# A two-layer mixer and mixture-of-experts trunk: smaller last block, both gates in the rows, twelve converted experts, and plain gathers at the second layer's start

## The reference

```python
def reference(x, ...):                      # x: (4, 4096, 1024) float32
    for l in range(DEPTH):                  # DEPTH = 2
        m = hybrid_mixer(x, ...)            # x @ w_in -> 2048 columns; four groups:
                                            #  gated 128-chunk mixing, 31-tap causal conv,
                                            #  trailing means of 2,4,8,16, 3-tap gated conv;
                                            #  RMS norm per group of 256, then @ w_o
        x = layer_norm(ALPHA * x + m, ln1_g[l], ln1_b[l])
        f = grouped_moe(x, router_w, router_b, exp_w_gate[l], exp_w_up[l], exp_w_down[l])
        x = layer_norm(ALPHA * x + f, ln2_g[l], ln2_b[l])
    return x

def grouped_moe(...):
    # 16 experts in 4 groups; the best group by the sum of its two best scores,
    # the top 2 experts in it, gates = softmax of their two logits
    for e in range(16):
        h = silu(xt @ w_gate[e]) * (xt @ w_up[e])      # 1024 -> 512
        y = y + dense_gates[:, e:e+1] * (h @ w_down[e])  # 512 -> 1024
```

## Time and profile before

| | |
|---|---|
| median of 3 runs | 2028.21 us (2025.96 to 2029.23) |
| profiled execution, time | 2037.57 us |
| its slowest core (core 2), span | 2036.5 us |
| the other cores' spans | 2007.5 to 2031.0 us |
| mean granted TensorE clock | 0.81 to 0.82 of full speed |
| busy share of the span | PE 62%, VectorE 51%, ScalarE 31%, GpSimd 24% |
| DMA moved | 334.99 MB, mean 164 GB/s |

### The profile page before, as it was taken

The page is one execution under the profiler, slowest core; times in us unless marked ns, Lnnn a source line. Parts: engine busy times, 40 slices in busy tenths (PEclk is TensorE's granted clock), DMA queues, the critical chain, the costliest instruction groups (busy, mean ns, idle before and its releaser), DMA issues.

```text
span 2036.5 us, 23801 instructions; the slowest of 8 cores (2007.5 to 2036.5 us)
## 1 busy us (share of the span) xinstructions
PE 1260.2 (62%) x7040; PEld 640.8 (31%) x7040; DVE 1041.5 (51%) x2328; ACT 637.1 (31%) x1109; POOL 496.1 (24%) x361
## 2 busy tenths in 40 slices
PE   0577868586429698685254687767535967878200
PEld 0433333232215454342121233333223534544000
DVE  1357486757733232232279658675761322323597
ACT  0344544435202222120254254443421211211122
POOL 4011315041340000001845112303031000000597
PEclk9897879798659899897567798978766989989655
DMA  9947667759848999997965878974124999997663
GB/s 199 260 137 99 99 94 125 104 89 180 160 123 208 260 224 249 246 236 222 206 134 64 112 93 115 125 89 90 63 84 144 236 244 230 247 256 168 225 210 131
DMA packets 78766, 334.99 MB, mean 164 GB/s; under 512 B 10776, under 2 KB 22688, under 8 KB 62880
## 3 DMA queue, kind: packets, MB, share of 16 engines
q0 software_dynamic: 26384, 166.16, 50.1%
q1 hardware_dynamic: 52240, 167.14, 25.3%
HBM read 362.71 MB, written 147.19 MB: 250 GB/s over the span
## 4 chain that ended last, share of the span: by engine, by line
PE 38%; DMA 17%; DVE 16%; issue 15%; ACT 8%; POOL 3%; DVEq 0%; SPq 0%; ACTq 0%; another core or an unknown queue 0%; POOLq 0%
PE pb L596 36%; DMA yg<-s_scr 6%; DMA s_wbuf<-ew 3%; DMA s_xy<-xg 3%; DMA s_xtok<-x 2%; ACT s_scr L605 2%; PE pT L1287 1%; ACT s_xy L641 1%; DVE s_sm L624 1%; ACT L605 1%; ACT s_xtok L605 1%; DVE s_scr L609 1%; DVE s_sm L675 1%; DVE s_scr L616 1%; DVE s_xtok L609 1%
## 5 line engine op out<-in xcount | busy, mean ns | idle before, releaser
L596 PE MATMUL pb<-s_xy,s_wbuf 128*128 128x352 bf16 (+2 forms) x2992 | 657.4, 349 | 145.2 <-ACT s_scr L605 34.5
L596 PEld LDWEIGHTS pb<-s_xy,s_wbuf 128*128 128x128 bf16 x2992 | 288.6, 104 | 396.3 <-issue 237.0
L596 PE MATMUL pb<-s_wbuf,s_scrb 128*128 128x512 bf16 (+1 forms) x768 | 232.1, 399 | 51.6 <-DMA s_wbuf<-ew 28.4
L616 DVE TENSOR_SCALAR s_scr<-pb,s_gsl 128x512 f32<-128x512 f32 (+1 forms) x192 | 135.6, 745 | 234.8 <-PE pb L596 167.6
L596 PE MATMUL pb<-s_wbuf,s_xy 128*128 128x512 bf16 x792 | 239.2, 412 | 8.9 <-DVE s_xtok L624 2.2
L609 POOL TENSOR_TENSOR s_xtok<-s_xtok,s_lnp 128x1024 f32<-128x1024 f32 x76 | 183.8, 2422 | 199.8 <-ACT s_xtok L605 153.4
L609 DVE TENSOR_TENSOR s_scrb<-s_scr,pb 128x352 bf16<-128x352 f32 x128 | 64.6, 519 | 229.9 <-PE pb L596 218.8
L406 POOL DMA_DIRECT2D s_wbuf<-exp_w x42 | 22.4, 532 | 645.8 <-PE pb L596 577.8
L641 ACT COPY s_xy<-pT 128x1024 bf16<-128x1024 bf16 (+1 forms) x96 | 90.3, 940 | 283.4 <-PE pT L1287 253.2
L1287 PE MATMUL pT<-s_identb,s_xy 128*128 128x128 bf16 (+1 forms) x768 | 121.9, 226 | 89.0 <-DMA s_xy<-xg 53.2
L709 PE MATMUL pT<-s_identb,s_scr 128*128 128x128 bf16 x336 | 55.0, 273 | 182.2 <-ACT s_scr L605 70.5
(11 more groups left out here) (119 smaller groups left out, 1619.2 us busy)
## 6 DMA issues: line engine op xcount, KB each, us to landing
ew<-exp_w POOLq DMA_DIRECT2D x36, 1536.0 KB, 17.8
s_wbuf<-ew SPq DMA_DIRECT2D x54, 1024.0 KB, 14.6
s_wbuf<-exp_w POOLq DMA_DIRECT2D x42, 1024.0 KB, 15.4
yg<-s_scr SPq DMA_DIRECT2D x64, 512.0 KB, 15.0
s_xy<-xg SPq DMA_DIRECT2D x32, 514.0 KB, 13.4
yg<-s_scr SPq DMA_DIRECT2D x32, 384.0 KB, 17.8
xg<-s_gov SPq DMA_DIRECT2D x2, 5808.0 KB, 31.4
s_xtok<-x SPq DMA_DIRECT2D x17, 512.0 KB, 10.6
```

What stands on the lines that cost most here:

```text
L596: em.op(PE, lambda e: e.matmul(out.ap, lhsT.ap, rhs.ap, start=start, stop=stop), w=[out], r=[lhsT, rhs])
L616: em.op(E, lambda e: e.tensor_scalar(out=out.ap, in0=a.ap, scalar1=a1, scalar2=None, op0=op0), w=[out], r=rr)
```

## The change

Four things are changed together.

1. The blocks become 384 (halo tile and two more), 512, 512, 512 and 256 tokens. In the second layer the first block is no longer cut down: its convolutions, pooling and projections run on all 384 columns, while `G_section`, `O0_section`, `A_section` and `R_section` take only its tiles 1 and 2 (`tiles_of`).
2. The rows of `xg` carry three float32 columns: the second gate, the difference of first and second gate, and the base slot of the first expert. They are written once per block, and all scatters of the block follow with no write between them. `x_turn` works out the gate of a slot by two VectorE operations (is the first expert this one? then add the difference) in place of one copy. Rows are loaded with 516 float32 words instead of 514.
3. `PRE` becomes every expert with e % 4 != 3: twelve instead of nine (5, 9 and 13 are new), in both layers. `NTOK` becomes 3, and a conversion counts 4 instead of 6 bytes an element in the scheduler's DMA model.
4. In the second layer, tiles 0 to 3 are gathered with eight plain gathers into four buffers in the `w_o` region of `wbuf` and added by `vt` (VectorE or GpSimd). The load of `w_o` (piece 4) moves behind them into the second layer's program; the pieces 0 to 3 stay at the end of the first.

```diff
-MBLOCKS = [(0, 128)] + [(128 + i * NB, NB) for i in range(TM // NB)]
+MBLOCKS = [(0, 384), (384, NB), (896, NB), (1408, NB), (1920, 256)]
-PRE = [e for e in range(NE) if e % 2 == 0 or e == 1]
+PRE = [e for e in range(NE) if e % 4 != 3]
-NTOK = 2
+NTOK = 3
...
-                       w=[ewD[l].rows(2 * e + h, 2 * e + h + 1), tok[k].rows(0, 1)], r=after, size=64 * 12288 * 6)
+                       w=[ewD[l].rows(2 * e + h, 2 * e + h + 1), tok[k].rows(0, 1)], r=after, size=64 * 12288 * 4)
...
+            def tiles_of(b):
+                t0, nb = MBLOCKS[b]
+                return list(range(1 if last and b == 0 else t0 // 128, (t0 + nb) // 128))
...
+                ts(DVE, gcol(0), c1(lb), -0.5, ALU.mult, 0.5, ALU.add)
+                cpy(DVE, gcol(1), c1(lb))
+                tt(DVE, v16(tmp), v16(eq1), e16(ebase()), ALU.mult)
+                rsum(la, tmp)
+                cpy(DVE, gcol(2), c1(la))
...
                 for k in range(2):
-                    xr, xf = xrow[b == nblk - 1], xrowf[b == nblk - 1]
-                    gcol = xf(0, nt * GW // 2).v(lambda ap: ap.rearrange("p (t c) -> p t c", t=nt)[:, :, D // 2:D // 2 + 1])
-                    gcol.box = xr[0](D, GW).box[:3] + (xr[nt - 1](D, GW).box[3],)
-                    cpy(DVE, gcol, ge.v(lambda ap: ap[:, k * nt:(k + 1) * nt].rearrange("p (t o) -> p t o", o=1)))
                     for t in range(nt):
...
             if l > 0:
+                stg = [View(wbuf, 16384 + k * 2 * D, F32, D) for k in range(4)]
+                for i in range(4):
+                    for k in range(2):
+                        c, g = k * NT + i, stg[(2 * i + k) % 4]
+                        gc = gai(2 * i + k, 2 * i + k + 1)
+                        em.gather(g().ap, ygD[l - 1].ap, gc.ap, "dg%d" % c, w=[g(), gtok.rows(i, i + 1)],
+                                  r=[ygD[l - 1].rows(0, NSLOT + 1), gc])
+                    for k in range(2):
+                        vt(xtile(i), stg[(2 * i + k) % 4](), xtile(i), ALU.add)
+                load_layer_weights(l, only=[4])
                 for (t0, nb) in MBLOCKS:
                     for k in range(2):
-                        for i in range(t0 // 128, (t0 + nb) // 128):
+                        for i in range(max(4, t0 // 128), (t0 + nb) // 128):
                             c_gather(k, i, ygD[l - 1])
...
-                gv = xgG[s](j * 514 + 512, j * 514 + 513)
-                cpy(DVE, gsl(s * CT + j, s * CT + j + 1, 0, nj), gv.v(lambda ap: ap[0:nj, :]))
+                gv = [xgG[s](j * 516 + 512 + q, j * 516 + 513 + q).v(lambda ap: ap[0:nj, :]) for q in range(3)]
+                gs_ = gsl(s * CT + j, s * CT + j + 1, 0, nj)
+                stt(DVE, gs_, gv[2], float(e * CAP), gv[1], ALU.is_equal, ALU.mult)
+                tt(DVE, gs_, gs_, gv[0], ALU.add)
...
-                load_layer_weights(l + 1)
+                load_layer_weights(l + 1, only=range(4))
```

More of the change, by code:

```diff
@@ L880, in build @@
             last = (l == n_layers - 1)
+            def tiles_of(b):
+                t0, nb = MBLOCKS[b]
+                return list(range(1 if last and b == 0 else t0 // 128, (t0 + nb) // 128))
             def G_section(b):
                 t0, nb = MBLOCKS[b]
[L883 to L884 removed]
+                tiles = tiles_of(b)
                 GS = 272
@@ L961, in CPS_section @@
                 t0, nb = MBLOCKS[b]
-                tiles = list(range(t0 // 128, (t0 + nb) // 128))
-                state_only = last and b == 0 and stop is None
                 accs = []
@@ L1225, in R_section @@
                     ts(DVE, flag(l, l + 1), m1.v(lambda ap: ap[:, 0:1]), float(CAP), ALU.is_gt)
-            skip0 = last and stop is None
             def C_section(b):
```

115 lines of the change are left out of this document (46 added, 69 removed).

## The result

The change makes the kernel slower. Its median is 2072.45 us (2066.89 to 2076.43, 4 runs) beside 2027.39 us for the kernel before (4 runs): a ratio of 1.022, 95% interval 1.0194 to 1.0245. The forecast was 1956 us, with a chance of 0.08 for slower. Some executions of a kernel run longer at a lower granted clock; medians and ratios here leave them out, which leaves e3 and e11 two runs and no interval, while the stage times of e5 come from such an execution, and the ratios of e13 to e16, which count one of the kernel before (2055.8 us), would be 0.003 higher without it. The slowest core is now core 5.

What follows compares the result with a forecast made beforehand. Expert stages were taken as near DMA and PE limits, mixers as bound by the PE, ACT and DVE chain. Terms -14 - 12 - 19 - 27 - 0 = -72 us, from 2028.2 to 1956 us; range 1920 to 2002.

Steps and rivals of the forecast that it cites:

- the price of the pace: Both mixers: cost of planning a conversion at 11.7 us; 5 us in the first mixer, hidden in the second.
- 200 us are free: hidden: Second mixer: DMA is busy 0.65 of 584 us, so six more conversions, 79 us per layer, cost nothing.
- the first rival: Conversions planned at 11.7 us but taking 13.2 block the POOL queue: 80 us in all, 2036 us, chance 0.08.
- The conversion's 13.2 us: DMA time of one conversion, worked out from the software queue's busy time with 12 us taken off for scatters.
- 430 to 450 us of work in 417: First mixer: conversions, scatters and loads exceed the time left, so 15 to 35 us spill into the first expert stage.
- Part 1 and 2, first mixer, -14 us: First mixer: blocks and gates save 23 us in the tail, less loading, router and conversion costs; bounds 0 and -30.
- Part 3, expert stages, -12 and -27 us: Expert stages: three more converted experts give -27 us each, less 15 us of spill in the first.
- Part 4 and the second mixer, -19 us: Second mixer: plain gathers and a fuller first block end the stage at 1526 against 1545; bounds +10 and -45.
- The first norm begins near 968: Start of the second layer: plain gathers and two adds let the first norm begin near 968 instead of 987.1.
- The second mixer gains nothing: Rival for the second mixer: DVE sets its pace, 1975 us in all, chance 0.15.
- The turnover of `wbuf`: Rival: it holds the expert stages, not DMA; -10 and 0 instead of -27 and -12, 1985 us, chance 0.17.
- the fourth rival: The expert stages come down to PE's floor: -40 in the second, -30 in the first, 1925 us, chance 0.15.

Runs made afterwards that it cites:

- e3: The changed kernel with a conversion counted as 6 bytes an element again, still twelve experts and three tokens: 2032.7 and 2034.2 us, no interval.
- e11: e5 with twelve converted experts in the second layer and nine in the first: 1966.5 and 1986.1 us, no interval.
- e5: e1 with the second layer's gathers put back to accumulating ones, so new blocks and gates only: 1978.5 us, ratio 0.975 to the kernel before.
- e13: The kernel before with only the planned cost of a conversion changed, 4 in place of 6: 2093.2 us, ratio 1.029.
- e16: e12 with the staged gathers as well, their adds and norms fixed on VectorE: 1951.6 us, ratio 0.960.
- e1: The changed kernel with part 3 undone (nine converted experts, two tokens, factor 6): 2016.5 us, ratio 0.989 to the kernel before.
- e4: The changed kernel with two tokens instead of three: 2091.3 us, ratio 1.024 to the kernel before.
- e8: The changed kernel with twelve tokens and twelve semaphores instead of three tokens: 2220.2 us, ratio 1.096 to the kernel before.
- e10: The kernel before with only the gates in the rows, on its old blocks and gathers: 1990.7 us, ratio 0.981.
- e9: The changed kernel with nine converted experts instead of twelve, keeping factor 4 and three tokens: 2086.7 us, ratio 1.030 to the kernel before.
- e12: e10 with twelve converted experts in the second layer only, factor 6 and two tokens: 1973.2 us, ratio 0.971 to the kernel before.
- e14: The changed kernel with a planned conversion cost of 5 in place of 4: 2003.0 us, ratio 0.985 to the kernel before.

## Why the prediction was wrong

By stage, the forecast was -14, -12, -19 and -27 us. The medians of the cores moved by +41, -45, +63 and -37. Both mixers went the other way, and the expert stages gained more than was forecast.

**The step that failed** is the price of the pace, which the sum put at 5 us for both mixers together. It stands in three places: "a price for the conversions on the POOL queue (part 3), 5 us" in the first mixer, "200 us are free: hidden" for the second, and the first rival, at 80 us in all and a chance of 0.08. The mechanism of that rival is what happened: POOL waits for conversions, and "the norm's multiplies, the adds and the scatters" stand behind. Measured, the two mixers lose 64 and 53 us to part 3 (after against e1), 117 in all; the planned cost alone, on the kernel before, costs 43 and 26 (e13). The rival's price was 1.5 us of lag for each of 52 conversions, and the trace shows 14.4 us for a planned 11.7: 2.7 us each, 140 us in all. That this is near 117 is not a confirmation of the sum, since POOL's waits were 369 us and only part of them reached the mixers. The two arguments against the rival fail. It names "three tokens instead of two": that does nothing (e4), and twelve are worse (e8). That "the real mixer gives more time than a plan without waits" was not enough: in e13 POOL waits 229 us. Free time of the DMA engines, counted over a stage, hides this: the second mixer's share was 0.65, and still only 0.73 in the changed kernel, where q0 is at 98% while conversions run.

**The conversion's 13.2 us** were worked out from a queue that was not full. In the full queue it is 14.2 us of DMA time and 14.4 from start to start with no scatter between, so the price itself was 1 us too low. By the Trainium skill (DMA: Bandwidth & Descriptors, Bandwidth) an estimate for its 4.7 MB is 13.2 us; the trace of the changed kernel is 8% above that. The sum that gave 430 to 450 us of work in 417 left out the 19 us of first expert pieces that it names: its terms give 450 to 470, and a spill of 32 to 52 us by its own numbers.

**Part 1 and 2, first mixer, -14 us.** Without part 3 it is -24 (e1), inside the bounds, but the sum was made of wrong terms. The gates were put at 11 us and give 21 (e10). The wider first and smaller last block were put at 8 net and give 2, which is nothing. The step looked at the tail alone and left out POOL's 7 us of wait for the same write in another block.

**Part 3, expert stages, -12 and -27 us.** The second's 27 is right in size: 29 against e9, 19 for e12 against e10. In the first the spill did not come with factor 4: the last conversion was issued at 557 us and the stage began only at 636, as the mixer had grown. The gain there was 24 against e9. With factor 6 the spill is real: e3's first expert stage is 391 us, 24 above the kernel before and 32 above e1. Some 7 us of the whole change's gain in this stage belong to part 4.

**Part 4 and the second mixer, -19 us.** The stage is 10 us longer without part 3 (e1). The earlier start of the gathers, put at 6.4 us, came true at 7 us. "The first norm begins near 968" was right in its start (18.7 us after the first gather in e1, for 25.7 before) and wrong in what follows: the norm's multiply was taken to be free to run, and stands on POOL behind the gathers. That tiles 0 to 3 come first was taken from the code; the planner mixes the order. The gates give 17 us there, where 3 were counted, since POOL's 18 us of waits in the middle blocks were left out; this hides how much the gathers cost.

**Beside the rivals.** "The second mixer gains nothing" holds for e1, and DVE's pace isn't shown as its cause: DVE is busy 398 of 598 us there. The turnover of `wbuf` doesn't hold the expert stages: three experts more give 19 to 32 us a stage, where the DMA time saved was put at 31. With the changes of the other parts they come down by 45 and 37 us, as far as in the fourth rival; but PE is busy 272 of 326 us, so they are not at its floor. The row named in advance as a sign of being wrong, POOL waits on `ew` over 40 us, is 389.

## What to carry to other kernels

A planned cost is part of the kernel: if an in-order engine issues transfers that a plan thinks shorter than they are, each one's shortfall delays what stands behind it on that engine and in that queue. Before changing such a number, take the distance between two successive transfers from a trace in which the queue is full, and keep the plan at or above it: here 14.6 for 14.4 us gave the second mixer its length back. Then look at what stands last in the queue. In e14 the last scatters, which the next stage waits for, landed behind the last conversions and cost 46 us more than in e1. When a step is moved to start earlier, follow each operation that the result needs through the queue of the engine it will run on. Change the parts one by one: here gates in the rows and twelve conversions in the second layer alone were worth 3%, hidden under one number that cost as much.

## What the runs showed that was not expected

- A conversion from DRAM to DRAM of 3.1 MB float32 into 1.57 MB bf16 keeps a distance of 14.4 us to the next when the queue is full, and 20.9 us with six scatters between.
- The landing time in the software queue goes with what stands ahead in it: scatters of 0.27 MB landed after 41 us with three conversions allowed in the queue, and after 172 us with twelve.
- More tokens, that is a deeper queue, made the kernel slower by 7% (1.022 to 1.096).
- The granted clock of the first mixer was 0.77 in the changed kernel, with PE busy 0.60 of it, for 0.81 at 0.66 before. In the second mixer it stayed at 0.76, though PE's share fell from 0.57 to 0.53.
